# Cached attention of a hybrid decoder step: half of the keys from a second, turned layout of the cache

## The reference

```python
past = cache_mla[e][page_table].reshape(Bd, past_len, LAT_DIM)
lat = jnp.concatenate([past_lat, rows], axis=1)
s = (jnp.einsum('bqhc,bkc->bhqk', q_lat, c_kv) + jnp.einsum('bqhr,bkr->bhqk', q_pe, k_pe)) * MLA_SCALE
p = jax.nn.softmax(s, axis=-1)
out = jnp.einsum('bhqk,bkc->bqhc', p, c_kv)
```

## Time and profile before

| what | us |
|---|---|
| median of 3 runs | 3082.57 |
| lowest and highest | 3078.41, 3083.43 |
| profiled execution, its time | 3076.06 |
| profiled execution, its span | 3074.3 |
| the stage's step loop in it | 434 (503 to 937) |

### The profile page before, as it was taken

One profiled execution on the slowest core, in us unless ns is written; L12 is line 12 of the kernel. 1 busy time (PEld: TensorE's weight loads), 2 busy tenths in 40 slices (PEclk: granted clock), 3 DMA queues, 4 the chain that ended last, 5 costly groups with the idle time before them and its releaser, 6 DMA issues. The chain is left out here.

```text
span 3074.3 us, 55978 instructions
## 1 busy us (share of the span) xinstructions
PE 2978.1 (97%) x22805; PEld 2769.3 (90%) x22805; DVE 1631.1 (53%) x2254; ACT 1263.9 (41%) x2187; POOL 1639.1 (53%) x1375
## 2 busy tenths in 40 slices
PE   8999999999999999998999999999999999989998
PEld 7999667777777999998999989998899999989998
DVE  4122465566554374547666626734445644576665
ACT  4111435656654344344444452312444334344443
POOL 1122103455441167878999715731111687789995
PEclk9999999999999999999999999999999999999999
DMA  6222204667663134446344134657541444454442
GB/s 225 56 81 75 65 28 161 213 231 243 220 251 108 49 112 153 143 133 218 136 152 146 43 127 149 227 205 281 200 123 45 142 145 133 152 200 141 144 144 80
DMA packets 298127, 451.91 MB, mean 147 GB/s; under 512 B 18545, under 2 KB 195633, under 8 KB 297617
## 3 DMA queue, kind: packets, MB, share of 16 engines
q1 hardware_dynamic: 277152, 357.54, 34.6%
q0 software_dynamic: 20000, 88.64, 8.3%
q10 hardware_dynamic: 720, 2.16, 0.2%
HBM read 318.47 MB, written 129.81 MB: 146 GB/s over the span
## 5 line engine op out<-in xcount | busy, mean ns | idle before, releaser
L112 PE MATMUL mlp_X<-mlp_f_hi,mlp_w_hi 128*128 128x272 f32 x1968 | 568.7, 289 | 15.8 <-DVE xT L965 14.0
L113 PE MATMUL mlp_X<-mlp_f_lo,mlp_w_hi 128*128 128x272 f32 x1968 | 568.9, 289 | 0.0
L114 PE MATMUL mlp_X<-mlp_f_hi,mlp_w_lo 128*128 128x272 f32 x1968 | 568.1, 289 | 0.0
L809 POOL TENSOR_TENSOR mlp_w_lo<-mlp_raw,mlp_w_hi 128x256 fp32r<-128x256 f32 (+1 forms) x348 | 344.2, 996 | 162.2 <-ACT mlp_w_hi L693 120.8
L112 PEld LDWEIGHTS mlp_X<-mlp_f_hi,mlp_w_hi 128*128 128x128 f32 x1968 | 371.6, 189 | 18.4 <-DVE xT L965 16.3
L113 PEld LDWEIGHTS mlp_X<-mlp_f_lo,mlp_w_hi 128*128 128x128 f32 x1968 | 372.0, 189 | 0.0
L114 PEld LDWEIGHTS mlp_X<-mlp_f_hi,mlp_w_lo 128*128 128x128 f32 x1968 | 371.7, 189 | 0.0
L809 POOL TENSOR_TENSOR mlp_w_lo<-mlp_sums,mlp_w_hi 128x256 fp32r<-128x256 f32 (+1 forms) x276 | 299.7, 1086 | 14.5 <-ACT mlp_w_hi L693 11.1
L112 PE MATMUL mlp_Z<-mlp_f_hi,mlp_w_hi 128*128 128x272 f32 x976 | 281.3, 288 | 3.8 <-ACT mlp_ev L732 2.2
L113 PE MATMUL mlp_Z<-mlp_f_lo,mlp_w_hi 128*128 128x272 f32 x976 | 281.5, 288 | 0.0
L114 PE MATMUL mlp_Z<-mlp_f_hi,mlp_w_lo 128*128 128x272 f32 x976 | 281.0, 288 | 0.0
(11 more groups left out here) (577 smaller groups left out, 7598.2 us busy)
## 6 DMA issues: line engine op xcount, KB each, us to landing
hidden<-mlp_ev SPq DMA_DIRECT2D x224, 272.0 KB, 2.2
mlp_f_lo_plain<-hidden SPq DMA_DIRECT2D x112, 544.0 KB, 5.5
mlp_raw<-in_w_down SPq DMA_DIRECT2D x64, 512.0 KB, 3.5
mlp_raw<-in_w_up SPq DMA_DIRECT2D x48, 512.0 KB, 5.6
projections<-odd_zout SPq DMA_DIRECT2D x24, 544.0 KB, 4.2
forms<-gla_f SPq DMA_DIRECT2D x20, 544.0 KB, 2.7
residual<-xT SPq DMA_DIRECT2D x2, 4352.0 KB, 15.1
projections<-even_zout SPq DMA_DIRECT2D x16, 544.0 KB, 3.2
```

What stands on the lines that cost most here:

```text
L112: pe.matmul(out, w_hi, x_hi, start=first, stop=False, skip_group_check=onto)
L113: pe.matmul(out, w_hi, x_lo, start=False, stop=False, skip_group_check=onto)
L114: return pe.matmul(out, w_lo, x_hi, start=False, stop=last, skip_group_check=onto)
L809: pool.tensor_tensor(to, x, y, op).then_inc(done_by, 1)
```

## The change

A second copy of the cache, `cache_turned`, is handed to the kernel. In it each page is stored turned: 128 partitions (value positions) of 320 values (the page's 128 tokens for positions 0 to 127, the same for 128 to 255, and the 64 rotary positions folded so that each half of the partitions holds 64 tokens). For groups 2 and 3 of each step (`COME`) the scores read these turned pages, which SyncE brings by page number: `fetch_keys(step)` reads 8 page numbers from a row of SBUF, one after another, and issues one DMA of 163,840 bytes for each into `kd`, which has two buffers. Groups 2 and 3 are still fetched by rows too, for the value product, whose wait for them moves there; their transposes and copies (units 5 to 9) go. The buffer of step n is refilled for step n + 2 when `score(n)` is done. SyncE's work for the recurrence is written as functions and called slot by slot, so that it stands between the page fetches. The query tile gets a seventh form. To make room, `v_own` (the samples' own values) and the page table move into `K.acc`, a tile that other stages use.

```diff
-    UNITS = 10
-    ACT_UNITS, DVE_UNITS = (0, 2, 4, 5, 7, 8, 9), (1, 3, 6)
+    COME = (2, 3)
+    NCOME = len(COME)
+    UNITS = 5
+    ACT_UNITS, DVE_UNITS = (0, 2, 4), (1, 3)
...
+        kd = s.sb("kd", [P, 2, 4 * NCOME, LAT])
-        q = s.sb("q", [P, 6, NB, Q])
+        q = s.sb("q", [P, 7, NB, Q])
-        v_own = s.sb("v_own", [NS, NB, P])
+        v_own = K.acc[0:NS, 0:NB * P].rearrange("p (b n) -> p b n", b=NB)
+        pages = K.acc_plain[NS:NS + 1, 0:NB * PAGES]
...
         def _(sp):
+            def fetch_keys(step):
+                if step >= 2:
+                    sp.wait_ge(scored, step - 1)
+                for n in range(NCOME):
+                    for i in range(4):
+                        c = step * 16 + 4 * COME[n] + i
+                        page = sp.value_load(pages[0:1, c:c + 1], min_val=0, max_val=K.cache_turned.shape[0] - 1)
+                        sp.dma_start(kd[:, step % 2, 4 * n + i, :],
+                                     K.cache_turned[bass.ds(page, 1), :, :].rearrange("a p c -> p (a c)")).then_inc(kd_in[step % 2], 16)
...
+            def next_gate(h):
+                if h:
+                    sp.wait_ge(b_made, h)
+                sp.dma_start(logf, K.z[row(Z_F, h + 1), :]).then_inc(f_in, 16)
+            def next_value(h):
+                store_o(h - 1)
+                sp.dma_start(vg[:], K.z[row(Z_I, h), :]).then_inc(v_in, 16)
...
+            def slot(n):
+                for h in range(HEADS):
+                    own_slot = n + LEAD - SLOTS * h
+                    if own_slot == 1 and h:
+                        next_state(h)
+                    if own_slot == 2 and h + 1 < HEADS:
+                        next_gate(h)
+                    if own_slot == 2 and h:
+                        next_value(h)
+                    if own_slot == 5:
+                        output_gate(h)
+                    if own_slot == 12 and h + 1 < HEADS:
+                        next_query(h)
+                    if own_slot == 14:
+                        store_state(h)
+            sp.dma_start(pages, K.page_table).then_inc(table_in, 16)
             sp.dma_start(newmask, K.c_newmask).then_inc(mask_in, 16)
             sp.dma_start(starts[:], K.c_starts).then_inc(h_const, 16)
+            sp.wait_ge(table_in, 16)
+            fetch_keys(0)
             sp.dma_start(levels[:], K.c_levels).then_inc(h_const, 16)
             sp.dma_start(own[:], K.c_own).then_inc(h_const, 16)
             sp.dma_start(vg[:], K.z[row(Z_I, 0), :]).then_inc(v_in, 16)
...
+            fetch_keys(1)
+            for n in range(-LEAD, 0):
+                slot(n)
+            for step in range(STEPS):
+                slot(2 * step)
+                if step + 2 < STEPS:
+                    fetch_keys(step + 2)
+                slot(2 * step + 1)
...
             def turn_keys(step, u):
                 b = bank(("k", step, u))
+                if u == 0:
+                    wait_rows(pe, step, 0)
+                    wait_rows(pe, step, 1)
                 for i in range(4):
-                    end = pe.transpose(b[:, i * P:(i + 1) * P], latents(step, 2 * side + i // 2)[:, col:col + P], K.ident[:])
+                    end = pe.transpose(b[:, i * P:(i + 1) * P], latents(step, i // 2)[:, col:col + P], K.ident[:])
...
             def score(step):
+                pe.wait_ge(kd_in[step % 2], 64 * NCOME * (step // 2 + 1))
...
+                        if j in COME:
+                            n = COME.index(j)
+                            col = c * P + (odd * 64 if c < 2 else 0)
+                            turned_in = kd[:, step % 2, 4 * n:4 * n + 4, col:col + 64]
+                            end = pe.matmul(out.rearrange("q (r g u) -> q r g u", r=2, u=32), q[:, 6 if f == 5 else c, b, :],
+                                            turned_in.rearrange("p g (r u) -> p r g u", u=32), start=(f == 0), stop=(f == len(FORMS) - 1))
+                        else:
+                            end = pe.matmul(out, q[:, f, b, :], keys[:, part_of, j * 256:j * 256 + 256], start=(f == 0), stop=(f == len(FORMS) - 1))
...
             def value(step):
                 pe.wait_ge(*emptied(("p", step)))
+                for j in COME:
+                    wait_rows(pe, step, j)
...
-                early = (2, 4, 5) if sigmoids_at(step) else (2,)
+                early = (2, 4) if sigmoids_at(step) else (2,)
...
+def turned_pages(cache):
+    pages = cache[0].reshape(-1, 32, 2, 2, LAT).transpose(0, 4, 3, 2, 1).reshape(-1, LAT, P)
+    out = np.empty((pages.shape[0], P, LAT), cache.dtype)
+    out[:, :, 0:P], out[:, :, P:2 * P] = pages[:, 0:P], pages[:, P:2 * P]
+    out[:, 0:ROPE, 2 * P:], out[:, ROPE:P, 2 * P:] = pages[:, 2 * P:LAT, 0:64], pages[:, 2 * P:LAT, 64:P]
+    return out
```

More of the change, by code:

```diff
@@ L1963, in even_mix_stage @@
         o_sample = O[:, 256 + 2 * NS:256 + 3 * NS]
-        mask_in = s.sem("mask_in")
+        mask_in, table_in = s.sem("mask_in"), s.sem("table_in")
+        kd_in = [s.sem(f"kd_in{i}") for i in range(2)]
         lat_in = [s.sem(f"lat_in{i}") for i in range(RING)]
@@ L2007, in bank_of, with wait_rows @@
             return KB[at[name] % KT]
+        def wait_rows(pe, step, j):
+            g = step * GR + j
+            if g >= M.AHEAD:
+                pe.wait_ge(lat_in[g % RING], 16 * (g // RING + (g % RING >= M.AHEAD)))
         def filled(name):
@@ new lines, in store_s0, with store_o, next_state @@
+            def store_s0(h):
+                sp.wait_ge(us_out, 2 * h + 2)
+                sp.dma_start(K.hgrn_sample[:, h, :, :].rearrange("b k v -> k b v"), s0[:]).then_inc(s0_stored, 16)
+            def store_o(h):
+                sp.wait_ge(final, h + 1)
+                sp.dma_start(K.mix[row(0, h), :], ho).then_inc(ho_stored, 16)
+            def next_state(h):
+                store_s0(h - 1)
+                sp.wait_ge(s0_stored, 16 * h)
+                sp.dma_start(s0[:], K.state_hgrn[0][:, h, :, :].rearrange("b k v -> k b v")).then_inc(s0_in, 16)
@@ L2649, in apply_gate, with slot @@
                 dve.tensor_tensor(ho, ho, vg[:], ALU.mult).then_inc(final, 1)
-            def has_running_sum(n):
-                return any(n + LEAD - SLOTS * h == 3 for h in range(1, HEADS))
-            def slot(n, last_keys=None):
+            def slot(n):
                 for h in range(HEADS):
@@ L2689, in _ @@
             dve.memset(q[ROPE:P, 2, :, :], 0.0).then_inc(q_made, 1)
-            dve.memset(q[0:ROPE, 3, :, :], 0.0).then_inc(q_made, 1)
+            for form in (3, 6):
+                dve.memset(q[0:ROPE, form, :, :], 0.0).then_inc(q_made, 1)
             dve.tensor_copy(q[:, 0:2, :, :], M.qs[:, 0:2, :, :, :].rearrange("p c b h t -> p c b (h t)")).then_inc(q_made, 1)
@@ L2722, in _ @@
                     copy_keys(step + 1, 3)
-                slot(2 * step + 1, lambda: copy_keys(step + 1, 6))
-                if later and not has_running_sum(2 * step + 1):
-                    copy_keys(step + 1, 6)
+                slot(2 * step + 1)
                 bank_slot(2 * step + 1)
@@ L4206 @@
     nc = bacc.Bacc("TRN2", target_bir_lowering=False, num_devices=1)
-    arrays = {f"in_{n}": np.ascontiguousarray(x) for n, x in {**inputs, **constants()}.items()}
+    arrays = {f"in_{n}": np.ascontiguousarray(x) for n, x in {**inputs, **constants(), "cache_turned": turned_pages(inputs["cache_mla"])}.items()}
     a = {n[3:]: nc.dram_tensor(n, x.shape, mybir.dt.from_np(x.dtype), kind="ExternalInput").ap()
```

64 lines of the change are left out of this document (21 added, 43 removed).

## The result

The changed kernel takes 3099.53 us in the median of 4 runs (3098.32 to 3101.16), against 3081.90 us of 4 runs of the kernel before beside it (3078.41 to 3083.43). The ratio is 1.0055, with a 95% interval of 1.0042 to 1.0068. It is 18 us slower where 40 us less were forecast. The profiled execution took 3098.32 us.

A forecast was written before the change was run, and what follows sets the result against it. The prediction took TensorE to bound the loop. Its terms, -71 (transposes) + 18 (row landing) + 6 (start) + 7 (past SyncE's waits) = -40 us, led to a forecast of 3042 us, range 3027 to 3057.

The forecast's parts named there:

- Past SyncE's waits: Second step of heads 1 to 3: pages issued behind SyncE's waits come 2.3 us late each time, 7 us lost.
- Transposes: all of it is on the path: TensorE's loop: 20 transposes fewer in each of 32 steps, 2.2 us a step, 71 us saved in all.
- the rival: TensorE's loop: the transposes were covered by something else; put aside because TensorE is busy for 98%, given no chance.
- Neither engine is the bound, so I count nothing: PSUM copies: ScalarE loses 4 copies (2.4 us) a step and VectorE one; counted as nothing.
- Start: Stage start: SyncE's table read and eight pages before the constants delay the first score, VectorE and GpSimd; 6 us lost.
- Row landing: Row groups transposed early in the next step: a landing of 7.1 us gives back 4.5 us a head, 18 us.
- a page costs SyncE: SyncE's stream: number load, register work and issue taken at 1.25 us a page, 10 us a step, under every forecast step.
- the slower rival: SyncE binds: load, register work and issue in series; at 1.9 us a page 60 us lost, 3143 us; chance 14%.
- turned scores: Scores of turned groups, moving operand in runs of 32 values: taken as no dearer than 381 ns; at most 90 us.
- the DMA share of the loop: DMA engines in the loop: a share of 0.85 or more was named as a sign of the forecast.
- the forecast's 355: TensorE's busy time in the loop: about 355 us was named as a sign, with the loop near 395 to 400.
- the second rival: The DMA engines bind: priced by share, 282 + 122, the loop takes 404 us, total 3059 us; chance 15%.

The follow-up runs named there:

- no_pages: The changed kernel without any fetch of turned pages; scores of groups 2 and 3 read the keys of groups 0 and 1: 3052.05 us, 0.9862 of before.
- Store_split: The changed kernel with the wait for the stored sample states and the state's load one step later: 3095.55 us, 1.0036 of before.
- order_only: The changed kernel with pages fetched ahead of the even slot's transfers, the stored states' wait left in place: 3092.69 us, 1.0031 of before.
- One_dma: The changed kernel with one DMA of eight consecutive pages a step, without page table or register loads: 3083.13 us, 1.0018 of before.
- Few_bytes: The changed kernel with each page's DMA bringing 16 of 128 partitions from step 2 on: 3070.93 us, 0.9969 of before.
- keys_first: The changed kernel with pages fetched before the recurrence's transfers and the stored states' wait a step later: 3072.57 us, 0.9981 of before.
- no_pages_keep_early: no_pages with VectorE's masked copy of the odd slot ahead of its gather and second key copy: 3035.47 us, 0.9819 of before.
- before_keep_early: The kernel before the change with VectorE's masked copy ahead of its gather and second key copy: 3087.51 us, 0.9991 of before.
- keys_const_first: keys_first with the recurrence's constants sent ahead of the first eight pages: 3070.75 us, 0.9973 of before.
- keep_early_few: keys_const_first with VectorE's masked copy ahead of its gather, and pages of 16 of 128 partitions from step 2 on: 3057.78 us, 0.9911 of before.

## Why the prediction was wrong

**"Past SyncE's waits", 7 us, is the step that failed.** The place was right, and the size was not: the hand-over steps lose 33.5 us, of which no_pages keeps 8.5, so some 25 are the pages'. The score's waits for pages there are 22.5 us. The reckoning had pages out at the start of the step plus 12 and in after 10 + 3. In the trace the store begins 1.5 us into the short step that begins at 606.1, pages start at 619.92, 13.8 us into it, and the score stands 35.2 us after its start where the forecast had 23 to 25. Four things were left out:

- The store of the sample states, whose landing SyncE waits for. I took SyncE's times from the earlier trace rows, which begin behind it. The load behind it comes 8.9 us after it, not 3.8. The pages are a small part of that: in no_pages the three waits for that store are 17.8 us, up to 6.7, against 24.3 and 8.4. Store_split and order_only show that with this wait gone SyncE stands in the running sum's, and the other way round.
- The queue behind SyncE. The four transfers of half a megabyte that it issues just ahead of the pages were in the earlier trace rows as issues and not as 2.2 MB (an estimate from their sizes) that the pages' queue has to carry first. One_dma shows it: pages issued whole at 611.05, score at 630.7.
- The landing of the pages beside the rows, which I took as 3 us. The one-for-one exchange was in my text (186 against 192) but used only for the rows, each of which lets a small piece through. Its other side is that each small piece waits for a row packet four times its size. Few_bytes and the packet counts show it.
- The half clock, which came in the stretch after TensorE had stood 4.9 us for the values. It was nowhere in the sum, as the earlier trace rows has 1.00. The table by stretches shows it; no run here takes it apart from the waits that bring it.

The next head's values are a term that the prediction put at nothing without naming it: they wait 10.3 us in the changed kernel, 13.8 in keys_first, 25.2 in order_only and 9.0 without pages.

**"Transposes: all of it is on the path", 71 us, was wrong too.** That TensorE was busy for 98% of the loop was no proof that its work could shrink by a sixth and the rest stay away. I put the rival aside by saying so in its own words: "without moving the next wait forward". The next wait was VectorE's masked copy, and "Neither engine is the bound, so I count nothing" looked at VectorE's busy time alone, not at where its instruction stands. No_pages gives some 40 us by its medians and ratio; with the copy moved no_pages_keep_early gives 55, and before_keep_early shows that the wait was covered before.

**"Start", 6 us.** It costs 11.4 us by the trace, 5.5 of them before the first score, about as forecast, and 5.9 in the first two steps. GpSimd and VectorE do stand for the constants, and the first eight pages do stand ahead of those, as the waits and SyncE's timeline show:

```profile
POOL mix_lat L2140 <- DMA mix_own<-in_c_own: 11.5, 1, 11.5
...
DVE xT L2619 <- DMA mix_own<-in_c_own: 8.6, 1, 8.6
```

```profile
494.21 8.08 SPq L2043 DMA_DIRECT2D mix_kd<-in_cache_turned  x8
502.34 0.43 SPq L2103 DMA_DIRECT2D mix_levels<-in_c_levels  x1
```

But keys_const_first, which lets them go first, wins nothing that can be told. What does show in the traces is the fetching one by one. From the last DMA that SyncE issues ahead of the stage (L1706) to the third score it is 36.7 us before, 49.5 in the changed kernel, and 40.7 in one_dma, which has the same bytes and no register loads; in the other kernels with pages it is 45.6 to 49.1. So about 9 of these 13 us hang on the page-by-page fetch. That is one trace each, and before_keep_early, whose start is that of before, has 40.7 too, so with one DMA for eight pages no loss at the start can be told.

**"Row landing", 18 us,** was mis-sized: the transposes wait 4.9 us for rows. A part of it rested on a wrong reading: the stretches of the earlier trace rows don't all run from score to score. By the scores the eight steps from 601.2 us on last 11.9, 12.6, 12.6, 15.2, 14.3, 14.2, 15.5 and 13.9 us, so the last is no short step, and its 1.5 us a head had no ground. With steps of 13.3 us, not 12, rows have more time than the forecast gave them; in no_pages_keep_early, whose dense steps are 12.2 to 12.4, rows hold TensorE for 6.9 + 2.0 us.

**Right:** a page costs SyncE 8.08 / 8 = 1.01 to 20.09 / 16 = 1.26 us (1.25 taken; the sixteen have a pause of 3.2 us among them), so SyncE doesn't bind by its sum and the slower rival's mechanism isn't this one; turned scores take the median 379 ns of the others; the DMA share of the loop is 0.89; the DMA engines don't bind the loop once the pages go out in time, as keep_early_few, with an eighth of the bytes, has the ratio of keep_early. TensorE's busy time times its mean clock is 352 us (374.34 x 0.94) and 356 in no_pages, near the forecast's 355. The 122 us that the second rival adds by share have no working in the prediction; 113 us raised as 246 is to 282 would be 130.

Laid out anew from no_pages: the profiled spans of it and of the changed kernel differ by 41.0 us, of which 25.0 are the hand-over steps (70.9 against 45.9), 7.2 the first score and 9.1 the first two steps (30.6 against 7.7 + 13.8 = 21.5), which leaves 0.3 us with the other sign for all else. By the ratios they differ by 60. The kernel before was itself 8 us slower on the chip of that set, and the profiled execution of no_pages the slowest of its four (3057.42). On that chip before_keep_early, which is as fast as before, has a loop of 435.6 us against 404.2 of no_pages, so 31.4 us come off in the loop; against the trace of before on the first chip it would be 22.9. So the 40 us that no_pages gives may be less on the first chip, and the sum closes only to about 20 us. That stays open.

## What to carry to other kernels

A term like "twenty instructions fewer on the busiest engine" needs a second look at each wait that they cover: list who would be waited for next, by place in the order and not by busy share. Before an in-order queue gets a stream with deadlines, walk through all that stands ahead of it at the worst point, the landing of its own stores included, and treat all of the waits and loads there together: with one wait gone the next one held SyncE, and with the pages put first another load came late. Small pieces that share DMA engines with large packets should be given the landing time of a queue that gets a fifth of the bandwidth (82 of 405 GB/s here), and behind what the same queue still carries, not that of a transfer on its own.

## What the runs showed of the hardware

- With 1.2 KB pieces on one queue and 4.6 KB packets on the other, the shared engines took 424 against 422 in 6 us: bytes went one to four, 82 GB/s for the small ones, and 350 GB/s for them 2 us later, alone.
- A page number read into a register, three register instructions and the issue of a DMA took SyncE 1.01 us (eight at 494.21) to 1.26 us (sixteen at 619.92, with a pause among them).
- A load issued behind 512 and 544 KB transfers on the same queue waited for them: pages issued from 619.92 on moved their first pieces at about 627, and one_dma's, issued at 611.05, were waited for until 630.7.
- A moving operand in runs of 32 float32 values, taken from four blocks, took 376 ns at the least and 379 in the median, as one in a row did.
- The granted clock was 0.99 while TensorE stood idle from 626.3 to 630.9 us and 0.50 in the next 2.4 us. Its products of 32 x 256 took 0.64 us at 641.32; the step had a mean clock of 0.80 and the next 0.86.
